# Attention queries: turned once as they are and split into high and low parts behind the turn, with the row maxima moved into the score operand by small DMAs

## The reference

```python
q = rmsnorm(q, q_norm); k = rmsnorm(k, k_norm)          # 8 query heads, 2 key heads, 64 wide
s = einsum('bqkgd,bskd->bkgqs', q, k) * HEAD_DIM ** -0.5
p = softmax(s)                                          # over 1024 latent + 128 cached keys
o = einsum('bkgqs,bskd->bqkgd', p, v)                   # context queries see the 128 context keys
```

## Time and profile before

| | before |
|---|---|
| runs, us | 1796.09, 1800.35, 1804.50 |
| median, us | 1800.35 |
| span of the profiled execution, us | 1797.0 |
| TensorE busy in the span | 1666.8 us, 93% |
| weight loads of TensorE | 1359.4 us, 76% |
| VectorE busy | 1006.6 us, 56% |
| ScalarE busy | 623.8 us, 35% |
| GpSimd busy | 930.8 us, 52% |
| mean granted clock of TensorE | 0.976 of full speed |

### The profile page before, as it was taken

One profiled execution on the slowest core, in us unless ns is written; L12 is line 12 of the kernel. 1 busy time (PEld: TensorE's weight loads), 2 busy tenths in 40 slices (PEclk: granted clock), 3 DMA queues, 4 the chain that ended last, 5 costly groups with the idle time before them and its releaser, 6 DMA issues. The chain is left out here.

```text
span 1797.0 us, 40805 instructions
## 1 busy us (share of the span) xinstructions
PE 1666.8 (93%) x17412; PEld 1359.4 (76%) x17412; DVE 1006.6 (56%) x1476; ACT 623.8 (35%) x1248; POOL 930.8 (52%) x856
## 2 busy tenths in 40 slices
PE   4999999989989999999749999999799889999998
PEld 2898999969976555558638989999699865555586
DVE  2655306467746777791126553064577467777921
ACT  4322310144444444460143223101344444444601
POOL 1003396079953978852210033960798539788522
PEclk8999999999999999999969999999999999999999
DMA  9301112210000001032292011122100000001322
GB/s 337 119 27 61 62 54 69 86 45 22 4 12 14 6 26 33 25 135 104 73 335 102 27 61 62 59 62 87 45 22 4 9 17 6 26 27 31 124 104 84
DMA packets 71246, 117.22 MB, mean 65 GB/s; under 512 B 10128, under 2 KB 42128, under 8 KB 71056
## 3 DMA queue, kind: packets, MB, share of 16 engines
q1 hardware_dynamic: 70128, 114.18, 18.6%
q10 hardware_dynamic: 928, 0.34, 0.1%
HBM read 95.03 MB, written 19.47 MB: 64 GB/s over the span
## 5 line engine op out<-in xcount | busy, mean ns | idle before, releaser
L1434 POOL TENSOR_TENSOR attn_accp<-attn_accp,attn_pr 128x1024 f32<-128x1024 f32 x110 | 269.5, 2450 | 42.3 <-ACT attn_pr L1500 36.5
L93 PE MATMUL ps<-h_hi,in_w_hi 128*128 128x384 f32 (+1 forms) x816 | 276.0, 338 | 5.0 <-DVE h_lo L456 4.9
L94 PE MATMUL ps<-h_lo,in_w_hi 128*128 128x384 f32 (+1 forms) x816 | 274.5, 336 | 0.0
L95 PE MATMUL ps<-h_hi,in_w_lo 128*128 128x384 f32 (+1 forms) x816 | 274.4, 336 | 0.0
L1704 DVE TENSOR_REDUCE attn_ql<-ps 128x1 f32<-128x1152 f32 x128 | 172.7, 1355 | 103.2 <-PE ps L1622 102.9
L1500 ACT ACTIVATE attn_pr<-ps 128x512 f32<-128x512 f32 x292 | 158.7, 595 | 170.5 <-PE ps L1666 161.7
L93 PEld LDWEIGHTS ps<-h_hi,in_w_hi 128*128 128x128 f32 (+1 forms) x816 | 150.1, 184 | 13.3 <-issue 6.7
L94 PEld LDWEIGHTS ps<-h_lo,in_w_hi 128*128 128x128 f32 (+1 forms) x816 | 150.2, 184 | 3.9
L95 PEld LDWEIGHTS ps<-h_hi,in_w_lo 128*128 128x128 f32 (+1 forms) x816 | 150.0, 184 | 3.9
L1665 PEld LDWEIGHTS ps<-attn_QH,attn_KH 128*128 128x128 f32 x292 | 55.4, 190 | 122.0 <-ACT attn_pr L1500 55.2
L1675 PE MATMUL ps<-attn_pr,z 128*64 128x512 f32 x520 | 139.5, 615 | 0.0
(11 more groups left out here) (253 smaller groups left out, 3653.5 us busy)
## 6 DMA issues: line engine op xcount, KB each, us to landing
in_w<-in_w_in SPq DMA_DIRECT2D x22, 1024.0 KB, 6.1
zz<-in_w_mod SPq DMA_DIRECT2D x8, 2048.0 KB, 13.9
gates<-in_gate SPq DMA_DIRECT2D x48, 192.0 KB, 1.9
z<-out_y SPq DMA_DIRECT2D x18, 512.0 KB, 4.9
attn_gt<-gates SPq DMA_DIRECT2D x34, 256.0 KB, 2.6
z<-in_x_sample SPq DMA_DIRECT2D x16, 512.0 KB, 5.6
z<-in_w_mod SPq DMA_DIRECT2D x4, 2048.0 KB, 10.0
out_w<-in_w_out SPq DMA_DIRECT2D x16, 512.0 KB, 7.0
```

What stands on the lines that cost most here:

```text
L93: nc.tensor.matmul(out, a_hi(i), b_hi(i), start=(i == 0), stop=False)
L94: nc.tensor.matmul(out, a_hi(i), b_lo(i), start=False, stop=False)
L95: last = nc.tensor.matmul(out, a_lo(i), b_hi(i), start=False, stop=(i == n - 1))
L1434: nc.gpsimd.tensor_tensor(acc, a, pr[:, n % 4], ALU.add).then_inc(pool_added, 1)
```

## The change

Queries are no longer split ahead of the turn. TensorE turns the four token tiles of a pair as they lie in `z`, both heads at once, with four transposes ("turn"). ScalarE rounds each head's 64 rows of the turned queries from PSUM into its rows of `QH`, and copies them from there to the other 64 rows. VectorE subtracts the rounded part from PSUM into `QL` ("low"). The row maxima go into a tile `mx`, and SyncE moves them into row 64 of `QL` by eight DMAs to a pair, each from 128 partitions of 4 bytes into 512 bytes of one partition. `QL` gets a third buffer. GpSimd's `split` and the tiles `qhh` and `ql` are gone. Two maxima of pair 2 are made between step 0 and slot 0, the turn of pair p stands in slot b-13 and its "low" in b-12, and some "o" items move by one or two slots. Pairs 0 and 1 are turned in steps 8 and 13 of the scan, with their "low" in scan steps 11 and 17. Seven blocks of the output weights are now asked for once the scores of the step before the last pair are done, and one once all scores are done.

```diff
 def attention_slots():
-    first = [("hi", 0, 0), ("hi", 0, 1), ("hi", 1, 0), ("hi", 1, 1), ("max", 0, 0, None), ("max", 0, 1, None)]
...
+    first = [("max", 0, 0, None), ("max", 0, 1, None)] + [("max", 1, 0, b) for b in range(4)]
+    first += [("turn", 2), ("max", 1, 1, 0), ("max", 1, 1, 1), ("low", 2), ("max", 1, 1, 2), ("max", 1, 1, 3)]
+    between = [("max", 2, 0, 0), ("max", 2, 0, 1)]
...
-        slots[b - 8].append(("hi", p, 1))
-        slots[b - 6 + (p == 2)].append(("lo", p, 0))
-        slots[b - 2].append(("lo", p, 1))
         if p >= 3:
-            slots[b - 12].append(("hi", p, 0))
+            slots[b - 13].append(("turn", p))
+            slots[b - 12].append(("low", p))
...
-        slots[8 + 2 * t].append(("o", t))
+        slots[8 + 2 * t if t < 4 else 9 + 2 * t + (t == CTX)].append(("o", t))
...
+        def row_of_maxima(p):
+            sp.wait_ge(mx_read, call_number[p, 1, None if p == 0 else 3] + 1)
+            for e in range(2):
+                for t in range(4):
+                    sp.dma_start(QL[HD:HD + 1, p % 3, e, P * t:P * t + P].bitcast(F32),
+                                 mx[:, p % 3, e, t:t + 1].bitcast(F32), allow_slow_non_contiguous=True).then_inc(row_in[p % 3], 16)
...
+        asks += [(-2 if p < 2 else slot_of["max", p, 1, 3], 0, p) for p in range(len(PAIRS))]
+        sp.wait_ge(o_out, NT)
+        for _, which, n in sorted(asks):
+            if which == 0:
+                row_of_maxima(n)
+            else:
+                gate(n)
...
-        split(2, 0)
...
+            if item[0] == "turn":
+                p = item[1]
+                is_turned(act, *item)
+                for e in range(2):
+                    nc.scalar.activation(of_head(QH, half(e), p, e), turned_queries(p, e), ACT.Copy).then_inc(q_high, 1)
+                act.wait_ge(q_high, 2 * p + 2)
+                for e in range(2):
+                    last = nc.scalar.activation(of_head(QH, half(1 - e), p, e), of_head(QH, half(e), p, e).bitcast(F32), ACT.Copy)
+                last.then_inc(q_ready, 1)
...
+    def query_turn(pe, p):
+        turn_start(pe, ("turn", p))
+        for b in range(4):
+            last = nc.tensor.transpose(ps[:, 7, P * b:P * b + P], query_block(p, b), m["ident"])
         last.then_inc(turned, 1)
...
+    def lows(dve, p):
+        dve.wait_ge(q_high, 2 * p + 2)
+        for e in range(2):
+            last = nc.vector.tensor_tensor(of_head(QL, slice(0, HD), p, e), turned_queries(p, e),
+                                           of_head(QH, half(e), p, e).bitcast(F32), ALU.subtract)
+        last.then_inc(turn_copied, 1)
...
             if kt == 0:
-                is_turn_copied(pe, "lo", p, 1)
+                is_turn_copied(pe, "turn", p)
+                pe.wait_ge(row_in[p % 3], 128 * (p // 3 + 1))
...
-QUERY_TURNS = (8, 10, 12, 14)
+QUERY_TURNS = (8, 13)
+EARLY_LOWS = (11, 17)
...
-        attn["queries_turned"](sp)
-        for k in range(6):
+        attn["last_pair_begun"](sp)
+        for k in range(KD - 1):
             w_block(k)
         attn["scores_done"](sp)
-        w_block(6)
-        w_block(7)
+        w_block(KD - 1)
```

More of the change, by code:

```diff
@@ L1280, in attention_slots @@
     slots[1].append(("osum",))
-    rank = {"max": 0, "recip": 2, "norm": 3, "gate": 3, "osum": 4, "oscale": 5, "hi": 6, "lo": 7, "sum": 8, "o": 9}
-    return first, [sorted(s, key=lambda x: rank[x[0]]) for s in slots]
+    rank = {"low": 0, "max": 1, "recip": 2, "norm": 3, "gate": 3, "osum": 4, "oscale": 5, "turn": 6, "sum": 8, "o": 9}
+    return first, between, [sorted(s, key=lambda x: rank[x[0]]) for s in slots]
 def attention(nc, io, m, l, ctx, memory, au_out, o_out, state_out_done):
@@ L1311, in attention @@
     ps, z, br, of = m["ps"], m["z"], m["br"], m["of"]
-    first, slots = attention_slots()
+    first, between, slots = attention_slots()
     gate_items = [x for s in slots for x in s if x[0] == "gate"]
@@ L1315, in attention @@
     turn = {}
-    for item in first + [x for s in slots for x in s]:
-        if item[0] in ("hi", "lo", "sum", "o"):
+    for item in [("turn", 0), ("turn", 1)] + first + [x for s in slots for x in s]:
+        if item[0] in ("turn", "sum", "o"):
             turn[item] = len(turn)
@@ L1334, in values, with query_block, half, turned_queries @@
         return z[:, CTX if k == KT_CTX else k, 640 + HD * g:640 + HD * g + HD]
-    def queries(p, i):
+    def query_block(p, b):
         if p == 0:
-            return z[:, CTX, 256 * i:256 * i + 256].rearrange("p (h d) -> p h d", d=HD)
+            return z[:, CTX, P * b:P * b + P]
         t0, g, hp = PAIRS[p]
         c0 = 256 * g + P * hp
[L1341 to L1346, removed]
+        return z[:, t0 + b, c0:c0 + P]
+    def half(e):
+        return slice(HD * e, HD * e + HD)
+    def turned_queries(p, e):
+        x = ps[half(e), 7, :]
+        return x.rearrange("p (g n c) -> p g n c", g=2, c=P) if p == 0 else x
+    def of_head(x, rows, p, e):
         if p == 0:
[L1348 to L1352, removed]
+            return x[rows, 0].rearrange("p g (n e c) -> p g n e c", e=2, c=P)[:, :, :, e, :]
+        return x[rows, p % 3, e, :]
     def call_bank(n):
@@ L1404, in sync @@
                 sp.dma_start(gt[:, n % 2, 0:w], io["gates"][OUT_BLOCKS[k], :, c0:c0 + w]).then_inc(g_in[n % 2], 16)
+        slot_of = {item: n for n, items in enumerate(slots) for item in items}
+        asks = [(slot_of[gate_items[n - 2]] if n >= 2 else -1, 1, n) for n in range(len(gate_items))]
+        asks += [(-2 if p < 2 else slot_of["max", p, 1, 3], 0, p) for p in range(len(PAIRS))]
[5 more added lines that the diff above has]
+                gate(n)
         sp.wait_ge(kv_out, 32)
     def gpsimd(pool):
[L1408 to L1421, removed]
         def add(n):
@@ L1466, in gpsimd @@
                                         ALU.pow).then_inc(o_root, 1)
[L1467 to L1471, removed]
     def scalar(act, out):
@@ L1507, in key_high @@
             last.then_inc(k_high, 1)
-        def query_high(p, i):
-            n = ASKS.index((p, i))
-            for e in range(2):
-                last = nc.scalar.activation(blocks(qhh[:, n % 4, :, HD * e:HD * e + HD], p).bitcast(F32R), queries(p, i), ACT.Copy)
-            last.then_inc(q_high, 1)
         def keys_turned(j):
@@ L1544, in scalar @@
         act.wait_ge(on_in, 32)
-        evict(("hi", 1, 1))
         act.wait_ge(state_out_done, 32)
-        for item in first[4:-1]:
+        for item in first:
             if item in SPREADS:
@@ L1551, in scalar @@
         exponentials(0)
-        evict(first[-1])
         for n, items in enumerate(steps):
@@ L1683, in tensor @@
         scores(0)
-        work(first[-1])
+        for item in between:
+            work(item)
         for n, items in enumerate(steps):
@@ L1709, in work @@
                 maximum(*item[1:])
+            elif item[0] == "low":
+                lows(dve, item[1])
             elif item[0] == "recip":
@@ L1754, in work @@
                 nc.vector.tensor_tensor(o, o, oss[:, t].unsqueeze(2).broadcast_to([P, 4, HD]), ALU.mult).then_inc(o_ready, 1)
-        for item in first[4:]:
+        for item in first + between:
             work(item)
```

88 lines of the change are left out of this document (31 added, 57 removed).

## The result

Four executions of the changed kernel took 1829.83 to 1836.04 us, median 1833.49; four of the kernel before, beside them, 1799.26. The ratio is **1.019 (95% interval 1.016 to 1.021): slower by 1.9%, 34 us**. The forecast was 1810.5 us, 10 us slower, with a range of 1784 to 1838: the direction was right and so was the new wait, the size was a third of what came. The profiled execution has a span of 1833.2 us, 36.2 more than that of before.

A forecast was written before the change was run, and what follows sets the result against it. TensorE, busy 116.4 of 117 us in attention, was taken to bound the kernel. Per layer 17.2 us lost (8.85 + 5.15 + 3.2) against 12.1 gained, +5.1, +10.2 for two: 1810.5 us, range 1784 to 1838.

The forecast's parts named there:

- prices: TensorE's attention steps: 2.14 us for scores and values; maxima add 0.52, a "lo" turn 0.45, an "o" 0.23, a "sum" 0.87.
- overlap (A): Rival on the row DMAs: issues overlap, L falls to 4.2 us, 1786 us; wholly overlapped 1780.5 us; chance 0.28.
- dearer issue (B): Rival on the row DMAs: an issue may take 1 us, L = 9.3, 1860 us; on the way there 1830; chance 0.15.
- L: Delay from a pair's last maximum read to its scores, through eight DMAs: 6.2 us, shortest 4.2, longest from rows 7.4.
- The rule of the Trainium skill: On the row DMAs: fixed cost near 2 us each, dispatch some 50 ns, which would make L 2.5 us.
- The gain: TensorE's attention slots: 21 turns removed, 9.45 us, and waits beside them, net 3.65 us; together 13.1 us per layer.
- ScalarE's burst: Four ScalarE copies at a stroke make the next exponentials 0.8 us late; 0.17 charged for each of six pairs, 1.0 us.
- what it waits for is lost in full: TensorE in attention: what it is relieved of is gained in full, what it waits for is lost in full.
- pairs 3 to 8: Scores waiting for the row: 1.15 us each for pairs 3 and 4, 1.4 for 5 to 7, 2.35 for 8; sum 8.85.
- The start: Pair 1's row, up to slot 0: there at 575.5 us against 572.3, 3.2 us lost per layer.
- "Nothing" for VectorE's subtractions: Two VectorE subtractions of 0.68 us, in a slot without maxima, cost nothing except for pairs 2 and 3.
- rival C: Queue or VectorE late, VectorE short of room in slots 6 to 13: maxima slip 1 us three times a layer, 1817 us; chance 0.05.

The follow-up runs named there:

- experiment 1: Changed kernel with each column of the row maxima sent by its DMA as soon as it is read; 1805.39 us, ratio 1.002 to the kernel before.
- experiment 6: On top of experiment 1, GpSimd's softmax adds cut to 16 of 1024 elements of a partition, sums left incomplete; 1781.93 us, ratio 0.991.
- Experiment 4: Changed kernel with useless matmuls on TensorE ahead of the row wait of pairs 1 to 8; 1820.27 us, ratio 1.011 to the kernel before.
- (5): On top of experiment 1, VectorE's gate of pair 0, scaling of tile 1 and extra gates moved to other slots; 1786.69 us, ratio 0.993.

## Why the prediction was right in direction and a third in size

**The mechanism held as far as it went.** The row's wait replaces the turns, 16 times as forecast and largest for pair 2; turns, maxima and "o" kept their prices; the train is issued at 0.62 us a DMA, lands in 2.0, and the rivals of overlap (A) and of a dearer issue (B) are out. (A's shortest L takes 0.37 us for an issue, which no row of the prediction shows; the lone gate of the earlier trace rows has 0.32.) The rule of the Trainium skill that the prediction weighed, a dispatch near 50 ns (page "DMA: Bandwidth & Descriptors", section "Anatomy of one DMA — SWDGE (gpsimd) path"), stands in a section on DMAs that GpSimd issues; the trains of 4.98 us for 8 and 10.13 us for 16 show that it can't be carried over to SyncE's queue. The landing of 2.0 us agrees with the fixed cost near 2 us that the Trainium skill gives there.

**The gain was right.** The turns and the waits beside them gave 13.05 us per layer against 13.1. Another 0.87 came from slot 28 of before, which has only a call of maxima and takes 3.53 us instead of 2.66. The prediction said that the prices come out the same wherever one looks, and missed it:

```profile
663.20 0.76 PE L1622 MATMUL ps<-attn_KH,attn_QH 128*128 128x384 f32 x3 [0.62 <-DVE attn_ql L1704]
```

TensorE waits there for a maximum that VectorE reads late, behind a gate with two SBUF inputs of 2.47 us, where the next one takes 0.67. It is the trouble of experiments 1 and 6, visible in the trace of before. In the changed kernel the wait for the row of pair 4, in slot 26, covers it; once that wait is gone (experiment 1) it is back, with 0.87, and with GpSimd's adds made small (experiment 6) it is gone. ScalarE's burst cost 0.15 for each of five pairs; 0.17 was charged for each of six.

**The step that failed is the price of a wait.** The prediction priced a wait of TensorE at its length: "what it waits for is lost in full". That is a lower bound. Behind the waits around step 0, behind those of pairs 2 and 8 (4.4 and 2.6 us) and behind three of the six of 1.8, a step or two ran at a clock of 0.50 to 0.79, and behind those of 1.2 to 1.4 none did. The table puts 7.8 and 9.8 us per layer on them (3.2 and 2.4 of it in slots 0 and 1), 17.6 of the 21.9 us that the forecast missed between scan and last scores. Experiment 4 shows it: no row sooner, 13 us back. The trace of before could have told. In layer 0 TensorE waits 1.54 us for the last maximum ahead of step 0, and the second scores of that step then take 0.63 each, against the 0.40 of later steps:

```profile
569.66 0.63 PE L1665 MATMUL ps<-attn_QH,attn_KH 128*128 128x512 f32 x1
570.09 0.63 PE L1666 MATMUL ps<-attn_QL,attn_KO 65*128 65x512 f32 x1
```

From 568.6 to 571.2 us the granted clock is 0.50. In layer 1 the same wait of 1.54 us has no slow step behind it (step 0 takes 1.50 us there and 2.57 in layer 0), so after a wait of that length it is not certain. The prediction read steps only in the stretch where TensorE hardly stood, and there the clock is 1.00.

**The waits themselves were somewhat mis-sized.** L was 6.5 instead of 6.2. For pairs 3 to 8 the cost was 11.3 us where 8.85 was forecast, for pair 2 5.45 where it was 5.15. The start came out on both sides of its 3.2, at 1.8 and 4.3. Its parts (a "low" among the maxima, the row of pair 1) are there. Ahead of the second of the two added maxima TensorE also waits 1.54 us for VectorE, but in front of slot 0 it still waits 0.8 and 1.8 for the row, so that wait is covered. The two layers differ for two reasons. Step 0 of the kernel before was itself 1.07 us longer in layer 0, at the lower clock. And the stretch ahead of step 0 was 1.0 us shorter than before in layer 0 and 0.4 longer in layer 1; it ranges from 37.9 to 40.4 us over all kernels here. So only the mean of the two, 3.05, can be held against the forecast.

**"Nothing" for VectorE's subtractions was true only under the waits.** The work that hid them in the changed kernel was the wait for the row. Experiment 1 took it away, and the waits for maxima rose from 6.1 to 18.3 us; moving VectorE's items (5) or freeing their port (6) brought 19 and 23 us. The prediction's rival C was this, priced at 1 us three times a layer, with the wrong cause: not room, but the length of a gate or a scaling beside GpSimd's adds.

**The other 4 us** lie ahead of the first scan and were not tested; they come and go between profiled executions of kernels alike there.

## What to carry to other kernels

Price a wait of TensorE at its length plus the slow steps behind it: here a wait of 1.8 us cost nothing or 1.6 us more, one of 2.6 us 1.5, one of 4.4 us 1.5 to 2.8. A result carried by many small DMAs behind one wait costs the sum of their issues, not one landing; sent each when its value was there, they gave 28 of the 34 us back. And when a wait is removed, read who had finished under its cover: VectorE's instructions with two SBUF inputs took up to six times as long beside GpSimd's adds, and where they stood decided whether the gain was seen.

## What was not expected of the hardware

- Filling a wait with matmuls that nobody reads made the kernel 13 us faster (1833.49 to 1820.27): the clock stayed at 1.00 in stretches that had 0.50 to 0.75.
- The issue of a 4-byte-per-partition DMA within SBUF takes SyncE's queue 0.62 us in a train and 0.47 alone (the median of 144 in the first experiment), and in a train that is as much as the 128 KB loads of the earlier trace rows take: between these two sizes the cost of an issue doesn't change.
- The same VectorE instruction, 256 elements of 128 partitions, took 0.41 us (its mean beside the small adds) or as much as 2.58 us beside the full ones.
